# The low halves of the weights moved by 64 bytes in SBUF, in a one-core kernel of three transformer layers

## What is computed

```python
z = jnp.einsum("bsd,de->bse", rmsnorm(x, g_mix[i]), w_in[i])
u = jax.nn.relu(jnp.einsum("bsd,df->bsf", h2, w_up[i]))
x = x + jnp.einsum("bsf,fd->bsd", u * u, w_down[i])
...
gu = h @ w_in
return (jax.nn.silu(gu[..., :D_FF_2]) * gu[..., D_FF_2:]) @ w_out
```

## Time and profile before

| | |
|---|---|
| median of 3 runs | 2167.99 us (2163.68 to 2168.05) |
| the profiled execution, its own time | 2162.32 us |
| its span, first to last instruction | 2160.5 us |
| mean granted TensorE clock | 0.987 of full speed |
| TensorE matmul busy | 2095.5 us, 97% of the span |
| TensorE weight load busy | 1697.5 us, 79% |
| VectorE busy | 1146.3 us, 53% |
| ScalarE busy | 816.6 us, 38% |

### The profile page before, as it was taken

How to read it: one execution, slowest core, us unless ns; L and a number is a source line. 1 busy time by engine, 2 the same in 40 slices (tenths; PEclk the granted TensorE clock), 3 DMA queues, 4 the chain that set the end, 5 groups by cost and what they waited for, 6 DMA issues and landing times. The chain is left out here.

```text
span 2160.5 us, 26090 instructions
## 1 busy us (share of the span) xinstructions
PE 2095.5 (97%) x10710; PEld 1697.5 (79%) x10710; DVE 1146.3 (53%) x1706; ACT 816.6 (38%) x1169; POOL 38.4 (2%) x34
## 2 busy tenths in 40 slices
PE   8999999999999999999999999999999899999998
PEld 6876678888888887787878888887786577888886
DVE  5674765542542579888846444324634736444423
ACT  4324753331232465542534222213325734322212
POOL 0120000000000000000100000000000000000000
PEclk9999999999999999999999999999999999999999
DMA  4220012223223222233122222222240031222221
GB/s 177 86 83 35 2 59 99 94 95 109 85 96 103 91 81 100 108 117 97 40 98 74 95 95 94 95 96 95 98 173 23 1 118 59 98 98 98 98 98 68
DMA packets 43111, 190.68 MB, mean 88 GB/s; under 512 B 15520, under 2 KB 16224, under 8 KB 22384
## 3 DMA queue, kind: packets, MB, share of 16 engines
q1 hardware_dynamic: 40656, 184.78, 25.0%
q10 hardware_dynamic: 2336, 4.23, 0.6%
HBM read 185.25 MB, written 3.74 MB: 87 GB/s over the span
## 5 line engine op out<-in xcount | busy, mean ns | idle before, releaser
L250 DVE TENSOR_TENSOR weights_low<-weights_raw,weights_high 128x2048 fp32r<-128x2048 f32 (+1 forms) x161 | 365.8, 2272 | 565.4 <-ACT weights_high L223 565.3
L441 PE MATMUL psum<-split,weights_high 128*128 128x512 f32 x1448 | 568.3, 392 | 8.3 <-PEq L146 4.2
L442 PE MATMUL psum<-split,weights_high 128*128 128x512 f32 x1448 | 564.6, 390 | 0.0
L443 PE MATMUL psum<-split,weights_low 128*128 128x512 f32 x1448 | 564.6, 390 | 0.0
L223 ACT CAST weights_high<-weights_raw 128x2048 fp32r<-128x2048 f32 (+1 forms) x161 | 304.0, 1888 | 545.3 <-PE psum L443 504.7
L441 PEld LDWEIGHTS psum<-split,weights_high 128*128 128x128 f32 x1448 | 272.2, 188 | 70.3 <-issue 8.4
L443 PEld LDWEIGHTS psum<-split,weights_low 128*128 128x128 f32 x1448 | 272.0, 188 | 57.4
L442 PEld LDWEIGHTS psum<-split,weights_high 128*128 128x128 f32 x1448 | 272.0, 188 | 56.0
L443 PE MATMUL psum<-hidden_high,weights_low 128*128 128x512 f32 x256 | 99.6, 389 | 0.0
L441 PE MATMUL psum<-hidden_high,weights_high 128*128 128x512 f32 x256 | 99.6, 389 | 0.0
L442 PE MATMUL psum<-hidden_low,weights_high 128*128 128x512 f32 x256 | 99.6, 389 | 0.0
(11 more groups left out here) (485 smaller groups left out, 3081.4 us busy)
## 6 DMA issues: line engine op xcount, KB each, us to landing
weights_raw<-in_weights SPq DMA_DIRECT2D x161, 1024.0 KB, 4.9
minus_c<-minus_c_rows ACTq DMA_DIRECT2D x16, 256.0 KB, 7.3
x_stream<-in_x SPq DMA_DIRECT2D x4, 512.0 KB, 7.1
gdn_in_grown<-gdn_rows SPq DMA_DIRECT2D x4, 512.0 KB, 4.7
chain_grown<-gdn_rows SPq DMA_DIRECT2D x4, 512.0 KB, 3.7
out<-end_results SPq DMA_DIRECT2D x8, 256.0 KB, 2.1
table<-rope_tables SPq DMA_DIRECT2D x1, 1024.0 KB, 12.0
weights_raw<-in_weights SPq DMA_DIRECT2D x1, 768.0 KB, 4.2
```

The costliest lines, as they stand in the source:

```text
L250: self.nc.vector.tensor_tensor(out=self.low_of(n)[:, 0:width], in0=self.raw[:, n % 2, 0:width], in1=self.high_of(n)[:, 0:width].bitcast(se ...
L441: nc.tensor.matmul(bank, wh, ah, start=first, stop=False)
L442: nc.tensor.matmul(bank, wh, al, start=False, stop=False)
L443: return nc.tensor.matmul(bank, wl, ah, start=False, stop=last)
```

## The change

The tile `weights_low` gets 16 float32 (64 bytes) more in front, which are not used, and `arena_offset` loses 64 bytes. So the low halves lie 64 bytes further on, at 64 modulo 512 from the activations. `const`, `gains` and `conv`, which lie between the two, also move by 64 bytes. `weights_raw`, `weights_high`, `x_stream`, `square_sum` and the arena (`early_low` with it) stay. No instruction is added, removed or put in another place on any engine; only addresses change.

```diff
@@ -29,6 +29,7 @@
 D_FF2 = 2816
 CHUNK = 2048
+LOW_OFFSET = 16
 SOLVE = 32
@@ -158,7 +159,8 @@
         self.high = enter(nc.sbuf_tensor("weights_high", [P, 2, CHUNK], f32r))
-        self.low = enter(nc.sbuf_tensor("weights_low", [P, 2, CHUNK], f32r))
+        low = enter(nc.sbuf_tensor("weights_low", [P, LOW_OFFSET + 2 * CHUNK], f32r))
+        self.low = low[:, LOW_OFFSET:].rearrange("p (s c) -> p s c", s=2)
@@ -419,7 +421,7 @@
         conv = enter(nc.sbuf_tensor("conv", [P, N_CONV], f32))
-        enter(nc.sbuf_tensor("arena_offset", [P, 40], f32))
+        enter(nc.sbuf_tensor("arena_offset", [P, 24], f32))
```

## The result

The changed kernel takes 2194.98 us (median of 4 runs, 2193.31 to 2197.67) beside 2166.6 us for the kernel before in its runs. The ratio is 1.0134, with a 95% interval of 1.0116 to 1.0152. The time lies inside the forecast range of 2150 to 2203, but the forecast said no change, and that was wrong.

The account below looks back on a forecast made before the run. The prediction took TensorE's row of matmuls at a fixed 226.7 ns pitch to bound the kernel. All address costs were taken as zero, giving 2167 us, near the median of earlier runs, with an 8-in-10 range of 2150 to 2203.

Parts of the forecast that it names:

- What bounds the kernel: Whole kernel: TensorE runs a row of matmuls at a fixed pitch of 226.7 ns, broken by short pauses at stage ends.
- No change of order, and nothing for VectorE: Nothing is added, removed or reordered; VectorE's subtraction, 2272 ns on average, writes halves 64 bytes further on at zero cost.
- `const`: Moving the constants by 64 bytes, including the identity used in transposes: taken as zero, at most 3.2 us for 700 transposes.
- the pitch of the 2240: Matmuls with a low half as stationary operand: zero added to their pitch, upper bound 4.6 ns.
- the two rows with a full or nearly full load: Trace rows at distances 256 and 192 (80 columns), with steady pitches of 226.9 and 226.4 ns, read as no cost.
- The rotary key: Natural trial in the trace: 24 matmuls at distance 256, steady pitch 226.9 ns, then a switch to 0 without loss.
- the forget gate: Natural trial in the trace: distance 192, 80 columns, settling at 226.4 ns; taken to cover bare alignment too.
- the decay columns: Natural trial in the trace: 16-column loads, distance up 64 bytes per product, 231.3 ns with no steady stretch.
- The slower rival: Mixed distances unsettle the row of matmuls: 2202 us if all pitches suffer, 2179 if only the low half's; 24%.
- The faster rival: Equal distances cost something now, as two reads colliding modulo 512; removing it gives 2141 us, or 2154 for half; 18%.
- The moving low halves: 308 matmuls with a low half as moving operand: taken as zero, at most 4.3 us for all three per product.
- The rule of the Trainium skill: TensorE's separate SBUF ports for moving operand and weight loads: by it the sum would be zero at any distance.

Follow-up runs that it names:

- const_64: Kernel before with only `const`, `gains` and `conv` moved by 64 bytes, both weight halves left at distance 0: 2161.39 us, ratio 1.0000.
- all_64: Kernel before with weights, constants, `x_stream` and the whole arena moved together by 64 bytes, all distances kept: 2162.23 us, ratio 0.9992.
- both_64: Kernel before with both halves of the weights moved 64 bytes further on, constants moving too: 2205.27 us, ratio 1.0189.
- pairs_64: Changed kernel with every second product issuing its three matmuls in reverse order, halving the changes of distance: 2194.18 us, ratio 1.0132.
- low_256: Changed kernel with the low halves 256 bytes further on instead of 64, arena moved by 512 bytes: 2163.73 us, ratio 0.9995.
- cut_end: Kernel before, third matmul's 128-column load cut to columns 0 to 111, so it ends 64 bytes early: 2193.64 us, ratio 1.0141.
- cut_start: Kernel before, third matmul's 128-column load cut to columns 16 to 127, so it starts at distance 64: 2162.6 us, ratio 1.0004.

## Why the prediction was wrong

**What bounds the kernel** was right. It is a row of matmuls at a fixed pitch, and the change shows in that pitch. **No change of order, and nothing for VectorE**, was right: L250, now L252, went from 2272 to 2271 ns. **`const`** at zero was right (const_64).

**The step that failed** is this one: "For the pitch of the 2240 I take zero, since the two rows with a full or nearly full load are nearer to what the change makes than the one with 16 columns." The rows were read rightly, but distances were counted from the start of the loads. From the end, both trials were at 0 modulo 256, like the full weight slices everywhere else. The rotary key ends at 256 + 512 = 768, the forget gate at 704 + 320 = 1024. The trace had no settled load with its end elsewhere. What it did have was the decay columns: their ends go through 64, 128, 192 and 0 in turn, and they ran at 231.3 ns. That bound, 4.6 ns on each pitch of a product, came within 10% of the 4.2 ns measured. That it came so near is partly luck: in the decay columns all three loads of a product are off alike and the distance changes from product to product, which isn't what the change makes. The sentence "so the bare alignment is covered too" was true and no help, since absolute alignment doesn't matter (all_64).

**The slower rival** had 24% for its two sizes. Its price for all pitches, 35 us, is near the 28.4 measured, and its form is right in one thing: a third of the loads costs some 60% of what all of them cost (one load 13 ns a product, three 21), so a neighbour's distance counts. Its mechanism, that a steady distance is enough to settle, fell with both_64, and pairs_64 and low_256 speak against it as well. Only at 192 was a steady distance cheaper than a mix. **The faster rival** had the idea of two reads that meet at one place modulo some number of bytes. The time depends on the distance indeed, but the aligned case, a load's end on the moving operand's start modulo 256, is the good one.

**The moving low halves** were bounded by 4.3 us. The last down projection's own 346 against 355 gives 5.9 ns a matmul, so 5.4 us on the 3 x 308 if the other such stages behave alike. The bound was a little low and the zero wrong.

**The rule of the Trainium skill** (TensorE: Matmul & The Clock Gate, Step-by-step: what each phase is for), that TensorE has two independent read ports and a load takes no read bandwidth from a running matmul, doesn't hold here if it is read as a statement on time. Where a load ends in relation to the moving operand changes the pitch from 226.6 to 230.8 ns (cut_end beside cut_start shows 231.3 and 226.6). The measurement decides.

**What stays open.** Why an end at a multiple of 256 is good isn't shown. A load that is read from its last column would explain why the end counts, but no run here looks at that order. Which point of the moving operand counts is open too: its 512 columns are 2048 bytes, so its start and its end are equal modulo 256, and the high and the low activation lie alike, so the operand that streams beside the load and the one that streams after it can't be told apart. Why 192 is cheap when all three loads are there and dear when one is, and why 224 is dear again, isn't shown. Nor is it shown why after each pause six to eight matmuls run at 231 to 233 ns even at the good distance, or whether the rule is the same for loads much narrower than 80 columns. The distances tried are multiples of 32 bytes, with the type float32r and 512 moving columns.

## What to carry to other kernels

In a kernel that is bound by back-to-back float32r matmuls, place the tiles so that each stationary slice ends at a multiple of 256 bytes from where the moving operand starts; an unused tile of a few bytes cost up to 2% here. A pad or a new small tile in front of a large one is not neutral. When a trace offers natural trials of a thing it doesn't show, write down every quantity in which they differ from the case to be forecast, the end as well as the start, before taking the nearest.

## What the runs showed of the hardware

- The pitch of float32r matmuls with 512 columns depends on the distance in SBUF between the load's end and the moving operand (counted here from its start), modulo 256 bytes: 226.6 ns at 0, 233.5 ns with all loads off by 64, at a granted clock of 1.00 in both.
- The absolute address did not matter (ratio 0.9992 with all tiles 64 bytes further on), nor did the start of the load (1.0004 when it alone is off by 64).
- With all three loads of a product alike, 64 bytes too far cost 1.89%, 64 bytes too short 0.77%. One load in three 64 bytes too short cost 1.41%, more than all three.
- The full weight loads keep their 188 ns in the kernels at 0, 32, 64 and 192, and at 128 they take 188 to 192 ns on average. The time appears in the distance from one matmul's start to the next.
